# Hybrid decoder step, one core: attention's outputs transposed inside its loop, projection and W's inputs begun earlier

## What is computed

```python
q, k, v = qkv_proj(rmsnorm(x), w_qkv, b_qkv, pos)      # 16 heads of 64, 4 KV heads
s = einsum('...qhgd,...khd->...hgqk', q, k) * HEAD_DIM ** -0.5     # banded, blocks of 128
s = where(mask, s, -inf)
m = maximum(max(s), sink); p = exp(s - m)
o = einsum('...hgqk,...khd->...qhgd', p / (sum(p) + exp(sink - m)), v)
x = x + o.reshape(..., 1024) @ w_o + b_o                # the projection
x = x + hier_moe(rmsnorm(x))                            # router, top 2 of 32 experts
# layer 1: S5 scan with a complex diagonal, whose tables (powers, W) are functions of its weights
```

## Time and profile before

| | |
|---|---|
| runs | 934.75, 937.96 and 1979.59 us, median 937.96 us |
| profiled execution, span | 923.8 us |
| PE busy | 768.5 us, 83% |
| DVE / ACT / POOL busy | 405.7 / 259.9 / 151.3 us |
| chain that ended last | PE 63%, DMA 11%, DVE 11%, ACT 6% |

### The profile page before, as it was taken

One profiled execution on the slowest core, in us unless ns is written; L12 is line 12 of the kernel. 1 busy time (PEld: TensorE's weight loads), 2 busy tenths in 40 slices (PEclk: granted clock), 3 DMA queues, 4 the chain that ended last, 5 costly groups with the idle time before them and its releaser, 6 DMA issues.

```text
span 923.8 us, 12813 instructions
## 1 busy us (share of the span) xinstructions
PE 768.5 (83%) x4895; PEld 481.0 (52%) x4895; DVE 405.7 (44%) x1001; ACT 259.9 (28%) x554; POOL 151.3 (16%) x233
## 2 busy tenths in 40 slices
PE   3899977999899898999733689799999888999730
PEld 2344445868545695555423567544345487555410
DVE  3378695867588370111128677301112162211118
ACT  6020034635111202322213355310014311322113
POOL 1020003000779001332110201000000001333110
PEclk9999996979999889999976899899999979999885
DMA  9462135000532898999869787780131296999946
GB/s 341 145 201 101 51 112 221 2 0 2 200 117 114 290 411 303 409 411 402 351 201 309 198 209 174 212 313 0 49 133 46 70 396 245 405 409 408 396 156 226
DMA packets 75381, 201.81 MB, mean 218 GB/s; under 512 B 14872, under 2 KB 29592, under 8 KB 74264
## 3 DMA queue, kind: packets, MB, share of 16 engines
q1 hardware_dynamic: 58360, 161.77, 48.7%
q0 software_dynamic: 9696, 19.75, 6.1%
q10 hardware_dynamic: 7264, 19.46, 5.8%
HBM read 171.64 MB, written 39.39 MB: 228 GB/s over the span
## 4 chain that ended last, share of the span: by engine, by line
PE 63%; DMA 11%; DVE 11%; ACT 6%; SPq 5%; issue 3%; POOL 0%; PEldq 0%; DVEq 0%; POOLq 0%; PEld 0%; ACTq 0%
PE PSUM L2049 14%; PE PSUM L1852 10%; PE PSUM L1637 8%; PE PSUM L1796 7%; PE PSUM L1873 5%; DMA RING<-in_moe_w_up 3%; PE PSUM L1840 3%; DMA RING<-in_attn_w_qkv 3%; DVE X L1515 2%; SPq L476 2%; PE PSUM L1727 2%; PE PSUM L1999 2%; PE PSUM L1995 2%; DVE XNT L773 2%; PE PSUM L1594 2%
## 5 line engine op out<-in xcount | busy, mean ns | idle before, releaser
L1637 PE MATMUL PSUM<-RING,XNT 128*128 128x512 f32 (+2 forms) x256 | 94.5, 567 | 4.3 <-DMA RING<-in_attn_w_qkv 3.6
L1852 PE MATMUL PSUM<-PH 128*64 128x256 f32 x448 | 85.6, 399 | 8.4 <-DMA PH<-in_moe_w_up 3.9
L671 POOL DMA_INDIRECT PH<-xn_scratch,PH x32 | 32.5, 1017 | 342.4 <-DVEq L1459 247.7
L2049 PE MATMUL PSUM<-PH,XNT 128*128 128x512 f32 (+1 forms) x220 | 88.1, 593 | 0.3 <-PE PSUM L2049 0.3
L1852 PE MATMUL PSUM<-RING,PH 128*64 128x256 f32 x384 | 69.4, 392 | 11.2 <-DMA PH<-in_moe_w_up 6.4
L1594 PE MATMUL PSUM<-ONES,IDENT 128*128 128x128 f32 x348 | 49.8, 314 | 24.1 <-DVEq L1518 23.9
L1490 DVE TENSOR_TENSOR PH<-PH,PSUM 128x128 f32<-128x128 f32 x32 | 9.2, 289 | 136.3 <-ACT PH L976 136.3
L1637 PEld LDWEIGHTS PSUM<-RING,XNT 128*128 128x128 f32 (+1 forms) x256 | 40.4, 177 | 53.9 <-issue 47.7
L1852 PEld LDWEIGHTS PSUM<-PH 128*64 128x64 f32 x448 | 51.6, 144 | 27.0 <-issue 11.9
L1796 PE MATMUL PSUM<-RING,PH 128*128 128x512 f32 (+1 forms) x160 | 62.6, 593 | 0.0
L1594 PEld LDWEIGHTS PSUM<-ONES,IDENT 128*128 128x128 f32 x348 | 48.8, 229 | 24.5 <-DVEq L1518 24.0
(11 more groups left out here) (378 smaller groups left out, 1366.7 us busy)
## 6 DMA issues: line engine op xcount, KB each, us to landing
PH<-in_moe_w_gate SPq DMA_DIRECT2D x28, 512.0 KB, 10.9
PH<-in_moe_w_up SPq DMA_DIRECT2D x28, 512.0 KB, 13.2
RING<-in_moe_w_gate SPq DMA_DIRECT2D x24, 512.0 KB, 11.5
RING<-in_moe_w_up SPq DMA_DIRECT2D x24, 512.0 KB, 16.0
RING<-in_moe_w_down SPq DMA_DIRECT2D x24, 512.0 KB, 16.3
PH<-in_moe_w_down SPq DMA_DIRECT2D x24, 512.0 KB, 14.8
RING<-in_attn_w_qkv SPq DMA_DIRECT2D x4, 1536.0 KB, 18.3
XNT<-in_moe_w_gate SPq DMA_DIRECT2D x12, 512.0 KB, 16.6
```

The costliest lines, as they stand in the source:

```text
L671: pool.indirect_dma_start(out=XG[:, i % 2, :], out_offset=None, in_=xn_d[layer], in_offset=bass.IndirectOffsetOnAxis(ap=IDX[:, i:i + 1], a ...
L1637: last = te.matmul(PSUM[lo:hi, b0 + col // 512, col % 512:col % 512 + n], XT[:, c, t * P:t * P + r], RING[:, c // 2, (c % 2) * QKV + col:( ...
L1852: last = te.matmul(PSUM[m * 64:(m + 1) * 64, 2 + i % 2, 0:2 * FF], XGT[:, i % 2, c, m * 64:(m + 1) * 64], gu[:, :, c, :], start=(c == 0), ...
L2049: last = te.matmul(PSUM[p0:p0 + r, 2 * (i % 2) + w, :], XT[:, c, t * P:t * P + r], slot(SLOT[q])[:, (2 * (c % 3) + w) * 512:(2 * (c % 3) + ...
```

## The change

1. **Transposes in the loop.** The outputs of a prompt's unit u are transposed in the loop, in iteration u+2 (unit 7 in iteration 11, since the sample's units use all of banks 6 and 7), by the new `turn(u)`: 2 transposes into the free half (columns 256 to 511) of the bank where the unit's products were. ACT copies them (`ot_evac`, 128x256) over that unit's queries in QT, which nothing reads any more. OT becomes OTP, in the place of QT, and OTS, in the place of QTS. `pv(i)` now also waits for the evacuations of all turns up to iteration i. Units 16 and 17 are turned among the projection's first matmuls.
2. **Projection begun.** `project(0, 0, 0)` stands in the last iteration but one. The sample's 8 transposes stand in the last one, and DVE copies the first half of them there. The other seven products of tile 0's first half follow the last `pv` at once, with no wait for a phase. The projection uses banks 0, 1 and 4, 5 in place of 4 to 7, and `xt_pe` uses bank 6 and 7 in place of 0 and 1.
3. **Phase 2** is left by PE, ACT and DVE without a drain and without a wait there (`leave_phase`). SP still waits for it ahead of the weights of slot 4, and POOL ahead of ER. ACT leaves after all 16 evacuations, so the phase is complete later in the program than before.
4. **W.** INW is loaded ahead of all experts, during attention, into the top of slot 7; TW1 and TW2 lie in the place of VC. DVE starts `w_block(0)` right after the sample's second copy.
5. **POOL** loads the router's weights and squares during attention, ahead of the end of phase 2 (EP lies over BQKV).
6. **BO** is loaded by ACT in the last iteration.

```diff
+        OTP = PH[:, 0:KC * SEQ].rearrange("p (c t) -> p c t", c=KC)
+        OTS = PH[:, KC * SEQ:KC * NTOK].rearrange("p (c t) -> p c t", c=KC)
...
-        INW = a.take(IN_F)
+        INW = PH[:, PH_F - IN_F:PH_F]
...
                         if layer == 0 and e < RS + XS and SLOT[q] == RS:
                             sp.wait_ge(phase, NENG * 2)
-                            sp.wait_ge(S("bb_out"), 32)
-                            sp.dma_start(INW, in_d).then_inc(S("ins_in"), 16)
...
+            sp.wait_ge(S("bb_out"), 32)
+            sp.dma_start(INW, in_d).then_inc(S("ins_in"), 16)
             experts(0)
...
-        XT_BANKS = {0: (0, 2), 1: (0,), 3: (4,)}
+        XT_BANKS = {0: (0, 2), 1: (6,), 3: (4,)}
...
+        TURNED = [u for u in range(NU) if UNITS[u][0] == "p"]
+        TURN_AT = {(u + 4 if u == 7 else u + 2): u for u in TURNED}
+        def leave_phase(eng):
+            eng.sem_inc(phase, 1)
...
+            def ot_evac(u):
+                bk, b, h = turn_place(u)
+                act.wait_ge(S("o_transposed"), TURNED.index(u) + 1)
+                nc.scalar.activation(OTP[:, 2 * h:2 * h + 2, b * P:(b + 1) * P],
+                                     PSUM[:, bk, 256:512].rearrange("p (c t) -> p c t", c=2), ACT.Copy
+                                     ).then_inc(S("ot_ready"), 1)
...
                 if i + 1 < NU:
                     exps(i + 1)
+                if i in TURN_AT:
+                    ot_evac(TURN_AT[i])
+            ot_evac(NU - 2)
+            ot_evac(NU - 1)
...
+                turned = len([j for j in TURN_AT if j <= i])
+                if turned:
+                    pe.wait_ge(S("ot_ready"), turned)
...
+            def turn(u):
+                pe.wait_ge(S("o_scaled"), u + 1)
+                for j in range(2):
+                    last = te.transpose(PSUM[:, bk, 256 + j * P:256 + (j + 1) * P],
+                                        O[:, b, h * 256 + j * P:h * 256 + (j + 1) * P], IDENT[:, :])
+                last.then_inc(S("o_transposed"), 1)
...
+                if i in TURN_AT:
+                    turn(TURN_AT[i])
             pv(NU - 1)
-            pe.wait_ge(S("scores_masked"), NU)
-            pe.wait_ge(S("o_scaled"), NU)
-            end_phase(pe, 2)
-            pe.wait_ge(S("ots_ready"), 2)
+            for c in range(1, KC):
+                last = project(0, 0, c)
+                if c == 2:
+                    turn(NU - 2)
+                if c == 5:
+                    turn(NU - 1)
```

More of the change, by code:

```diff
@@ L202, in build @@
         RHO = a.take(HG * PCH).rearrange("p (g j) -> p g j", g=HG)
+        TW1, TW2 = a.take(BP * P), a.take(BP * P)
         EP = a.take(6 * 2 * GP).rearrange("p (n r g) -> p n r g", n=6, r=2)
@@ L205, in build @@
         EQ = a.take(2 * 2 * GP).rearrange("p (b r g) -> p b r g", b=2, r=2)
[L206 removed]
+        assert a.at - 19 * GP >= at_bqkv and a.at <= XBASE - (KC + 1) * 36
         a = Area(XBASE - (KC + 1) * 36)
@@ L1378, in _ @@
                 norm_dve(dve, ch, 1, t)
+            dve.wait_ge(phase, NENG * 2)
             end_phase(dve, 3)
@@ L1761, in _ @@
                     scores(i + 2)
+                elif i + 2 == NU:
+                    pe.wait_ge(S("scores_masked"), NU - 1)
+                    pe.wait_ge(S("ot_ready"), 4)
+                    project(0, 0, 0)
+                else:
+                    pe.wait_ge(S("scores_masked"), NU)
+                    for b in range(2):
+                        for j in range(4):
+                            last = te.transpose(PSUM[:, 2 + b, j * P:(j + 1) * P], OD[b][:, j, :], IDENT[:, :])
+                        last.then_inc(S("od_transposed"), 1)
                 p_transpose(i)
@@ L1806, in _ @@
                     logits_pe(pe, 0, t - 2)
+            pe.wait_ge(phase, NENG * 2)
             pe.wait_ge(S("wo_done"), NT)
```

83 lines of the change are left out of this document (44 added, 39 removed).

## The result

The changed kernel takes 925.94 us in the median of 20 runs (916.29 to 928.91), the kernel before, beside it, 926.79. The record's ratio is 0.9952, with a 95% interval of 0.9931 to 0.9974: 4.5 us faster, between 2.4 and 6.4. It is not the quotient of the medians, which are only 0.85 us apart; the plain means of the runs, without the one of 1979.59 us, are 924.9 and 928.6, which is 3.7 us. The forecast was 7.4 us, or 0.8%. A second and a third set of 12 runs give 0.995 (0.9923 to 0.9977) and 0.9953 (0.9916 to 0.9989). Ratios and differences rest on executions within 1.5% of their kernel's fastest; the traces of `after_again` (934.56 us) and `inw_late` (940.38 us) are of executions above that, so no difference is read from these two alone.

A forecast was written before the change was run, and what follows sets the result against it. PE's projection (241.63 to 309.76 us) was taken as the bound. Tail 16.8 - 6.5, less 0.5 for ACT's copy and 1.9 for turns, gains 7.9; the gather costs 0.5: 937.96 - 7.4 = 930.5 us, range 923.5 to 936.5.

The forecast's parts named there:

- No stall, with half a microsecond to spare: PE at the projection's normalised tiles 0 and 1: DVE has them ready at 260.0 and 275.3, PE asks at 261.2 and 275.8.
- the wrong 14.2 us: Level of the forecast: the median taken as 14.2 us above the profiled span, giving 937.96 - 7.4 = 930.5 us.
- The turns: Transposes of outputs put into the attention loop: 0.22 us each where PE is full, lengthening the loop by 1.9 us.
- ACT's copies: ACT's copies of the transposed outputs in attention: 0.39 us each, hidden, except one ahead of the last pv, 0.5 us once.
- The tail: From the last products to the end of tile 0's first half: 16.8 us before, 6.5 after, with nothing waited for.
- DVE keeps up, barely: DVE's W blocks beside the projection: block 2 waits for block 0's store, starts at 249 against 252.16; PE isn't stalled.
- rival C: DVE becomes the bound: W's block 0 store lands late and PE waits at tiles 0 and 1; 934 us, chance 0.17.
- POOL and SP: Squarings beside attention pay only for the tables; SP's later loads start at 304.3 and cost the first gather 0.5 us.
- The clock: PE's clock in attention: transposes raise it as other work does, so the added ones don't hurt it, against the skill's rule.
- A: PE's clock falls in the attention loop, low from iteration 12 to the end: 949 us, slower; chance 0.06.
- B: The low clock stretch near 196 to 206 us in attention goes, worth some 5 us: 925.5 us; chance 0.12.
- E: The change does nothing, since the experts' loads bound the kernel and an earlier projection waits for them: 938 us; chance 0.03.

The follow-up runs named there:

- after_again: The changed kernel unaltered, run again for a second trace and ratio: 0.995 (0.9923 to 0.9977) to the kernel before.
- inw_late: The changed kernel with W's inputs (INW) loaded behind phase 2 again: ratio to the kernel before 1.0021 (0.9987 to 1.0056).
- store_first: The changed kernel with SP storing W's blocks 0 and 1 ahead of phase 2's wait and the four weight loads: ratio to before 0.9946 (0.9914 to 0.9977).
- squares_late: The changed kernel with POOL's router loads and squarings behind phase 2 again: ratio to the kernel before 0.9997 (0.9966 to 1.0029).
- before_again: The kernel before unaltered, run against itself for a second trace: ratio 1.0007 (0.9966 to 1.0048).
- double_turn: The changed kernel with each turn's two transposes made twice: steps of 4.27 us, against 4.05 in the changed kernel; no total time given.
- before_cut_b: The kernel before, ended ahead of the scan (behind the first mixture of experts), second time: median 505.8 us over 6 runs.
- before_scan_cut: The kernel before without the second mixture of experts and the final norm, ended behind the gated units: median 752.3 us over 5 runs.

## Why the prediction was right or wrong

**The size and the sign.** A gain of 4.5 us where 7.4 was forecast. The path was right (the projection is PE's, and what brings its first product forward brings its end forward), but the condition "as long as DVE keeps up" failed: the step that failed is "No stall, with half a microsecond to spare". The sum had the stall at nothing, and it measured 1.34 us. Two smaller misses stand beside it: the loop, +2.93 for +2.4, and the gather, -0.47 for +0.5. The last 1.4 us, from the 5.9 of the traced gather to the 4.5 of the times, are not explained; the spread of traced loops is larger than that. The chances by 2% hold (same), and the time of 925.94 lies in the range, but partly by accident: the level rested on the wrong 14.2 us. On the right 2 us the same sum gives 923.8 - 7.4 + 2.1 = 918.5 for the execution profiled, under the range, and 926.79 - 7.4 = 919.4 for the median, under all but two of the 20 runs. I had also written that 2% is about what a measurement of this kernel can tell. With 20 runs it tells 0.2%, so "same" was the wrong word for what I forecast myself: a change of 0.8% that shows.

**The turns** were right: 0.22 us each, 4.05 us a step, PE full. The loop and the wait behind it took 2.93 where I had 2.4. The seven steps that I had priced at 1.5 grew by 1.3, and the turn and the wait ahead of the last products took 0.8. What I had at nothing is iteration 10, which has no turn: from its transposes (at 190.88, now 191.83) to the next ones (202.28, now 204.02) it was 11.40 us, and is 12.19. Of the eight pairs of the sample's products there five take 1.22 us each at the low clock, where four did, and the pause ahead of them is 1.37 us in place of 1.26. Iteration 11's turn stands at 207.66, where the clock is high again. Whether the 0.8 us is the change's or chance, a single pair of traces can't say.

**ACT's copies** were right, 0.36 to 0.38 us each and hidden: ACT still waits 1.14 us for the next transposes, where I had about 0.8. The one at the end cost 0.56 where I had 0.5.

**The tail** was right in its mechanism, and its -10.3 came out at -8.63. 1.34 of the 1.67 us that are missing are the stall of the next paragraph, and `store_first` gave 1.53 of them back.

**DVE keeps up, barely.** This is the step that failed: DVE didn't, by 1.34 us, and it was the store of W's block 0 that held it up. DVE was ready for block 2 at 246.16 and waited 4.88 us, as forecast in kind. The store landed at 251.04 in place of 249: phase 2 ended at 240.2, not 239.3, and the store landed 8.94 us after its issue, itself 2 us behind the phase. And from block 2 to the normalised tile DVE took 10.93 us where it had taken 9.73. I had moved POOL's wide operations forward for tile 1 and forgotten that tile 0 gets them: L1126 takes 1.02 at 252.36, where the same operation takes 0.69 at other places, with POOL's 128x256 products beside it, and the sum X + bias (L1393) takes 1.76 us at 255.86 beside those of 128x512, where it took 1.25 before. The Trainium skill (SBUF — State Buffer, Who interferes with whom) says that a VectorE instruction with two SBUF inputs and a GpSimd instruction that reads SBUF exclude each other for their length. The trace agrees: L1126 reads SBUF twice and grows, L1125 beside it has an input in PSUM and stays at 0.68. At tile 0 the sum had 1.2 us of room (260.0 against 261.2), and half a microsecond at tile 1. The tile was normalised at 263.3, 3.3 us late, and PE asked for it at 262.1, 0.9 us late. So the room was an estimate with an error of 3 us, and rival C, which I gave 0.17, came in part: at tile 0, and not at tile 1.

**POOL and SP.** "That pays only for the tables" was the wrong step with the greatest consequence, though it didn't move the sum: without early squarings nothing of the gain is left (`squares_late`), because W's later stores stand behind the tables in one queue. The +0.5 for the gather didn't come (-0.47). SP's loads start at 307.36, not 304.3, because DVE and with it W's stores were late; they are 2.7 us nearer to the gather than before, and it takes 6.95 us all the same (7.01 before). So the term for shared DMA engines is not seen in this trace.

**The clock and A.** From 208 on it is 1.00 in all units with turns. Ten transposes a unit in place of eight (a quarter more, not the fifth that I wrote) left the granted clock at 1.00, so the rule on transposes that I weighed against the change had no effect here. A is refuted as an effect of the turns: where the low level did last into iteration 12, in `inw_late`, it did so in `before_again` too, which has no turns. **B**: the low stretch stayed in the changed kernel's traces. It is missing in `store_first` and `double_turn`, as chance from one execution to the next. And it is worth less than the 5 us of B: from iteration 10's transposes to iteration 13's `store_first` takes 18.97 us without it and the changed kernel 21.3 to 21.9 with it, 2 to 3 us, since PE then waits elsewhere (1.37 us for DVE, 0.75 for ACT). **E** is refuted: the gather moved by 5.9 us.

## What to carry to other kernels

When work is pulled forward, each of its inputs has to come forward with it, and the queue that stores its outputs too: here the turns with the early projection alone cost 5 us, the early inputs alone gave nothing that could be told, and either input left behind took the gain. Follow a queue's entries behind the one that you think of, for the squarings fed the tables, and W's stores stood behind those. And where a sum leaves half a microsecond of room in one place, put the expected stall into the sum; then look for the edit that makes the room. Here two such edits took 2.3 us from the traced path, and the times show no less.

## What the runs showed of the hardware

Behind a pause of 3.63 us of PE the clock was at 1.2 GHz, for some 3 us of extra time, and likewise behind one of 5.22 (eight transposes in 1.94 us) and one of 2.81 (`squares_late`, granted clock 0.50 from 301 to 303, and the last tile's 32 products in 8.70 us in place of 7.09). Behind pauses of 0.56 and 1.34 us it stayed high in the places shown. Inside attention a pause does not settle it: in the trace of before the low stretch follows one of 1.26 us, with the clock still high for 2 us behind it, but in `before_cut_b` and `before_scan_cut` the clock stays at 1.00 for 8 us and more behind the same pause, and in `store_first` it doesn't fall at all behind one of 1.37. That low stretch began and ended at different units in executions of one and the same kernel: the loop of before took between 76.4 and 80.8 us.

A store of 512 KB landed 8.94 us after its issue behind four loads of 512 KB, where the eight stores of W's blocks in that trace took 3.1 us in the median; ahead of the loads, in `store_first`, DVE did not wait for it. One traced execution is a poor base for a sum of a few microseconds unless its low stretches are those of the other.
